# Attention keys kept per head with the other head's rows zero, and a 64-column operand for the meta values

## The reference, cut to what matters

```
z = einsum('bhtd,bhsd->bhts', q_blk, k_pre) * d ** -0.5
valid = (s_pos < t_pos) & (s_pos >= PAD)
log_not = where(valid, log_sigmoid(-z), 0)
after = cumsum(log_not, axis=3, reverse=True) - log_not
a = where(valid, exp(log_sigmoid(z) + after), 0)
out = einsum('bhts,bhse->bhte', a, v_pre)
```

## Time and profile before

| what | value |
|---|---|
| median of 3 runs | 2059.4 us (2056.85 to 2059.65) |
| the profiled execution | 2060.28 us, span 2058.5 us |
| TensorE matmuls | 1997.3 us busy, 97% of the span |
| VectorE | 1095.7 us, 53% |
| ScalarE | 710.2 us, 35% |
| GpSimd | 14.6 us, 1% |
| mean granted TensorE clock | 0.976 |
| chain that ended last | 85% on TensorE, 8% VectorE, 4% ScalarE |

### The profile page before, as it was taken

The page is one execution under the profiler, slowest core; times in us unless marked ns, Lnnn a source line. Parts: engine busy times, 40 slices in busy tenths (PEclk is TensorE's granted clock), DMA queues, the critical chain, the costliest instruction groups (busy, mean ns, idle before and its releaser), DMA issues.

```text
span 2058.5 us, 25213 instructions
## 1 busy us (share of the span) xinstructions
PE 1997.3 (97%) x10194; PEld 1671.5 (81%) x10194; DVE 1095.7 (53%) x1346; ACT 710.2 (35%) x845; POOL 14.6 (1%) x10
## 2 busy tenths in 40 slices
PE   7999999989999999999999999999999999999996
PEld 6878888878989888898768888887898768888885
DVE  3444646454364554636554454454699664545445
ACT  5554646533232232333332222223423442222222
POOL 0000000000000000000000000000000000000000
PEclk9888989989999999999999999999999999999998
DMA  4001101012212222212312232222122112232231
GB/s 166 23 23 39 62 20 61 21 55 99 87 68 82 71 82 92 81 63 80 124 64 82 102 102 82 102 102 82 61 83 82 42 61 94 90 102 102 82 103 41
DMA packets 23474, 157.53 MB, mean 77 GB/s; under 512 B 2672, under 2 KB 3056, under 8 KB 5360
## 3 DMA queue, kind: packets, MB, share of 16 engines
q1 hardware_dynamic: 23408, 156.59, 22.1%
HBM read 154.48 MB, written 2.10 MB: 76 GB/s over the span
## 4 chain that ended last, share of the span: by engine, by line
PE 85%; DVE 8%; ACT 4%; issue 2%; DMA 1%; DVEq 0%; SPq 0%; ACTq 0%
PE psum L464 27%; PE psum L465 26%; PE psum L466 26%; PE psum L596 2%; PE psum L518 2%; DVE z L1291 2%; DVE normed L1291 1%; DVE h L1320 1%; PE psum L584 1%; ACT w_hi L856 1%; DVE w_lo L1284 1%; ACT std L856 1%; DMA w_raw<-in_units 0%; PE psum L617 0%; ACT X_hi L856 0%
## 5 line engine op out<-in xcount | busy, mean ns | idle before, releaser
L464 PE MATMUL psum<-X_hi,w_hi 128*128 128x512 f32 (+1 forms) x1632 | 603.4, 370 | 5.9 <-DVE X_lo L1300 5.0
L465 PE MATMUL psum<-X_lo,w_hi 128*128 128x512 f32 (+1 forms) x1632 | 596.3, 365 | 0.0
L466 PE MATMUL psum<-X_hi,w_lo 128*128 128x512 f32 (+1 forms) x1632 | 595.5, 365 | 0.0
L856 ACT ACTIVATE w_hi<-w_raw 128x2048 fp32r<-128x2048 f32 x140 | 267.4, 1910 | 411.8 <-PE psum L466 395.3
L1284 DVE TENSOR_TENSOR w_lo<-w_raw,w_hi 128x2048 fp32r<-128x2048 f32 x138 | 315.9, 2290 | 144.4 <-ACT w_hi L856 144.4
L464 PEld LDWEIGHTS psum<-X_hi,w_hi 128*128 128x128 f32 x1632 | 307.7, 189 | 64.2 <-issue 6.7
L465 PEld LDWEIGHTS psum<-X_lo,w_hi 128*128 128x128 f32 x1632 | 307.6, 189 | 49.2 <-issue 2.2
L466 PEld LDWEIGHTS psum<-X_hi,w_lo 128*128 128x128 f32 x1632 | 307.2, 188 | 49.4
L1429 DVE TENSOR_TENSOR acc<-acc,psum 128x512 f32<-128x512 f32 x216 | 142.0, 684 | 86.7 <-PE psum L466 86.7
L464 PE MATMUL psum<-M_hi,w_hi 128*128 128x512 f32 x352 | 136.9, 389 | 0.0
L465 PE MATMUL psum<-M_lo,w_hi 128*128 128x512 f32 x352 | 136.9, 389 | 0.0
(11 more groups left out here) (237 smaller groups left out, 2658.4 us busy)
## 6 DMA issues: line engine op xcount, KB each, us to landing
w_raw<-in_units SPq DMA_DIRECT2D x140, 1024.0 KB, 4.8
h<-in_xfm SPq DMA_DIRECT2D x4, 528.0 KB, 5.4
h<-in_xfm SPq DMA_DIRECT2D x1, 2112.0 KB, 7.5
decay<-in_dec SPq DMA_DIRECT2D x4, 512.0 KB, 4.7
out<-h SPq DMA_DIRECT2D x4, 512.0 KB, 2.8
rot<-in_consts SPq DMA_DIRECT2D x1, 528.0 KB, 11.6
acc<-in_consts SPq DMA_DIRECT2D x1, 448.0 KB, 9.0
vec<-in_vecs SPq DMA_DIRECT2D x1, 108.0 KB, 3.7
```

What stands on the lines that cost most here:

```text
L464: nc.tensor.matmul(dst, w2[0], x2[0], start=first, stop=False, skip_group_check=True)
L465: nc.tensor.matmul(dst, w2[0], x2[1], start=False, stop=False, skip_group_check=True)
L466: m = nc.tensor.matmul(dst, w2[1], x2[0], start=False, stop=last, skip_group_check=True)
L856: return nc.scalar.activation(out_, in_, f, **kw)
```

## The change

`K_hi` and `K_lo` get a further dimension, the head r: in the part for head r only that head's 64 rows are written, and the other 64 rows are zero. They are cleared once, by four memsets on GpSimd at the start, and never written again. `scores` multiplies over all 128 rows of the keys of head r and of the queries (both heads' rows). `key_hi` and `key_lo` write each head's rows by an instruction of their own, on 64 partitions.

`XM_hi` and `XM_lo` have 64 columns (X's first 32, twice) in place of 128, so the meta part of the value strip writes 64 PSUM partitions. `VM`, `VM_hi` and `VM_lo` are worked on in 64 partitions, and GpSimd clears the upper 64 partitions of `VM_hi` and `VM_lo` at the start. TensorE waits for all six memsets (`keys_padded`) ahead of its first call of `scores`; the memset of `acc` is queued behind them. `KM`, `KM_hi`, `VM`, `VM_hi` and `VM_lo` move to a place in SBUF that is otherwise used later by `sig`.

```diff
--- before.py
+++ after.py
@@ -37,6 +37,7 @@
 FULL = META + SEQ
 HALF = FULL // 2
 X_PITCH = 576
+XM_COLS = 64
 UNIT = 2048
 RET_HEADS, RET_DK, RET_DV = 4, 256, 512
 QUADS = 4
@@ -177,25 +178,27 @@
 
     rot = sb("rot", [P, 2, FULL])
     mixer = ExitStack()
+    quad_small = ExitStack()
+    KM = sb("KM", [P, P], F32, quad_small)
+    KM_hi = sb("KM_hi", [P, P], F32R, quad_small)
+    VM = sb("VM", [P, 2, P], F32, quad_small)
+    VM_hi = sb("VM_hi", [P, 2, P], F32R, quad_small)
+    VM_lo = sb("VM_lo", [P, 2, P], F32R, quad_small)
+    quad_small.close()
     sig = sb("sig", [P, 2, FULL], where=mixer)
 
     quad = ExitStack()
     Q_hi = sb("Q_hi", [P, 2, SEQ], F32R, quad)
     Q_lo = sb("Q_lo", [P, 2, SEQ], F32R, quad)
-    K_hi = sb("K_hi", [P, 2, SEQ], F32R, quad)
-    K_lo = sb("K_lo", [P, 2, SEQ], F32R, quad)
+    K_hi = sb("K_hi", [P, 2, 2, SEQ], F32R, quad)
+    K_lo = sb("K_lo", [P, 2, 2, SEQ], F32R, quad)
     V_hi = sb("V_hi", [P, 2 * BLOCKS, 3, SB_DH], F32R, quad)
     V_lo = sb("V_lo", [P, 2 * BLOCKS, 3, SB_DH], F32R, quad)
-    XM_hi = sb("XM_hi", [P, DT, P], F32R, quad)
-    XM_lo = sb("XM_lo", [P, DT, P], F32R, quad)
+    XM_hi = sb("XM_hi", [P, DT, XM_COLS], F32R, quad)
+    XM_lo = sb("XM_lo", [P, DT, XM_COLS], F32R, quad)
     XM2 = sb("XM2", [P, DT, 2, META], F32R, quad)
-    KM = sb("KM", [P, P], F32, quad)
     KM_x = sb("KM_x", [P, 2, META], F32, quad)
-    KM_hi = sb("KM_hi", [P, P], F32R, quad)
     KM_lo = sb("KM_lo", [P, P], F32R, quad)
-    VM = sb("VM", [P, 2, P], F32, quad)
-    VM_hi = sb("VM_hi", [P, 2, P], F32R, quad)
-    VM_lo = sb("VM_lo", [P, 2, P], F32R, quad)
     sp = sb("sp", [P, PACKED], F32, quad)
     sp_hi = sb("sp_hi", [P, PACKED], F32R, quad)
     sp_lo = sb("sp_lo", [P, PACKED], F32R, quad)
@@ -282,6 +285,7 @@
     x_loaded = sem("x_loaded")
     decay_loaded = sem("decay_loaded")
     memset_done = sem("memset_done")
+    keys_padded = sem("keys_padded")
     stored = sem("stored")
 
 
@@ -294,8 +298,8 @@
     post_done = sem("post_done")
 
 
-    qk_act = Steps(sem("qk_act"), ["K_hi", "KM_hi", "Q_hi"])
-    qk_dve = Steps(sem("qk_dve"), ["K_lo", "KM_part", "KM", "KM_lo"])
+    qk_act = Steps(sem("qk_act"), ["K_hi0", "K_hi1", "KM_hi", "Q_hi"])
+    qk_dve = Steps(sem("qk_dve"), ["K_lo0", "K_lo1", "KM_part", "KM", "KM_lo"])
     mk_act = Steps(sem("mk_act"), ["m_abs", "m_exp", "m_ln", "m_hi", "am_exp", "am_hi"])
     mk_dve = Steps(sem("mk_dve"), ["m_sp", "m_lo", "am_lo"])
     mk_pe = Steps(sem("mk_pe"), ["m_scores", "m_rows", "y_meta"])
@@ -447,6 +451,17 @@
         nc.gpsimd.memset(ones[:, :], 1.0).then_inc(ones_ready, 1)
         pool.wait_ge(x_lo_ready, DT)
         nc.gpsimd.memset(KM[:, :], 0.0).then_inc(memset_done, 1)
+        pool.wait_ge(memset_done, 1)
+        for r in range(2):
+            other = slice(SB_DH * (1 - r), SB_DH * (2 - r))
+            for n, x in enumerate((K_hi, K_lo)):
+                if r or n:
+                    pool.wait_ge(keys_padded, 2 * r + n)
+                nc.gpsimd.memset(as_f32(x[other, :, r, :]), 0.0).then_inc(keys_padded, 1)
+        for n, x in enumerate((VM_hi, VM_lo)):
+            pool.wait_ge(keys_padded, 4 + n)
+            nc.gpsimd.memset(as_f32(x[XM_COLS:P, :, :]), 0.0).then_inc(keys_padded, 1)
+        pool.wait_ge(keys_padded, 6)
         pool.wait_ge(cmat_ready, 1)
         nc.gpsimd.memset(acc[:, :, :], 0.0).then_inc(memset_done, 1)
 
@@ -546,7 +561,7 @@
             for nb, col, x in parts:
                 for k in range(DT):
                     end = x is parts[-1][2] and k == DT - 1
-                    mm3(psum[:, at.bank(s) + nb, col:col + 256], (x[0][:, k], x[1][:, k]),
+                    mm3(psum[0:x[0].shape[2], at.bank(s) + nb, col:col + 256], (x[0][:, k], x[1][:, k]),
                         (w[0][:, k, :], w[1][:, k, :]), k == 0 and col == 0, k == DT - 1,
                         (strip_done, 1) if end else None)
 
@@ -575,12 +590,10 @@
             pe.wait_ge(strip_free, at.strip(s) + 1)
             if not (type(g) is int and g == 0):
                 pe.wait_ge(hd_act.sem, hd_act.at("a_part2", g - 1))
-            rows = slice(SB_DH * r, SB_DH * (r + 1))
-
             for b in range(BLOCKS):
                 dst = psum[:, 4 + KEY_BANK[b], KEY_COL[b]:KEY_COL[b] + KEY_LEN[b]]
-                mm3(dst, split(K_hi, K_lo, rows, t, slice(b * P, (b + 1) * P)),
-                    split(Q_hi, Q_lo, rows, t, slice(b * P, SEQ)), b < 3, False)
+                mm3(dst, split(K_hi, K_lo, ALL, t, r, slice(b * P, (b + 1) * P)),
+                    split(Q_hi, Q_lo, ALL, t, slice(b * P, SEQ)), b < 3, False)
                 m = nc.tensor.matmul(psum[:, 4 + KEY_BANK[b], KEY_COL[b]:KEY_COL[b] + P],
                                      cmat[:, C_IDENT, :], cmat[:, C_BLOCKED, :], start=False, stop=False,
                                      skip_group_check=True)
@@ -690,6 +703,7 @@
         unit(at, 0, 0, "P", SEQ, from_x, [1])
         pe.wait_ge(cmat_ready, 1)
         pe.wait_ge(quad_ready, 6)
+        pe.wait_ge(keys_padded, 6)
         scores(0, 0, at, 1, 0)
         meta_scores(0, 0)
         quad_body(Place("quad_first"), 0, False, True)
@@ -956,7 +970,9 @@
 
         def key_hi(t, at, s, p):
             strips(at, s)
-            a(K_hi[:, t, :], psum[:, at.bank(s), :], ACT.Copy).then_inc(*qk_act.step("K_hi"))
+            for r in range(2):
+                own = slice(SB_DH * r, SB_DH * (r + 1))
+                a(K_hi[own, t, r, :], psum[own, at.bank(s), :], ACT.Copy).then_inc(*qk_act.step(f"K_hi{r}"))
             act.wait_ge(qk_dve.sem, qk_dve.at("KM", p))
             a(KM_hi[:, :], KM[:, :], ACT.Copy).then_inc(*qk_act.step("KM_hi"))
 
@@ -972,7 +988,7 @@
                 .then_inc(*v_act.step(f"V_hi{half}"))
             if half == 0:
                 act.wait_ge(strip_free, at.strip(0) + 1)
-                a(VM_hi[:, :, :], VM[:, :, :], ACT.Copy).then_inc(*v_act.step("VM_hi"))
+                a(VM_hi[0:XM_COLS, :, :], VM[0:XM_COLS, :, :], ACT.Copy).then_inc(*v_act.step("VM_hi"))
 
         def y_hi(t, p):
             act.wait_ge(y_out, p + 1)
@@ -1021,8 +1037,8 @@
             a(x[:, :, 1, :], ones[:, 0:SB_DH].unsqueeze(1).broadcast_to([P, 2 * BLOCKS, SB_DH]), ACT.Copy,
               scale=0.0).then_inc(quad_ready, 1)
         for x, y in ((XM_hi, X_hi), (XM_lo, X_lo)):
-            a(x[:, :, :].rearrange("p k (j m) -> p k j m", j=4),
-              as_f32(y[:, :, 0:32]).unsqueeze(2).broadcast_to([P, DT, 4, 32]), ACT.Copy).then_inc(quad_ready, 1)
+            a(x[:, :, :].rearrange("p k (j m) -> p k j m", j=2),
+              as_f32(y[:, :, 0:32]).unsqueeze(2).broadcast_to([P, DT, 2, 32]), ACT.Copy).then_inc(quad_ready, 1)
         first_hi(1)
         key_hi(0, at, 0, 0)
         query_hi(0, at, 1)
@@ -1384,9 +1400,11 @@
             v.tensor_tensor(Y_lo[:, t, :], Y[:, :], as_f32(Y_hi[:, t, :]), ALU.subtract).then_inc(y_lo_ready, 1)
 
         def key_lo(t, at, s, p):
-            dve.wait_ge(qk_act.sem, qk_act.at("K_hi", p))
-            v.tensor_tensor(K_lo[:, t, :], psum[:, at.bank(s), :], as_f32(K_hi[:, t, :]), ALU.subtract)\
-                .then_inc(*qk_dve.step("K_lo"))
+            for r in range(2):
+                own = slice(SB_DH * r, SB_DH * (r + 1))
+                dve.wait_ge(qk_act.sem, qk_act.at(f"K_hi{r}", p))
+                v.tensor_tensor(K_lo[own, t, r, :], psum[own, at.bank(s), :], as_f32(K_hi[own, t, r, :]),
+                                ALU.subtract).then_inc(*qk_dve.step(f"K_lo{r}"))
 
 
             KM_rows = KM[:, 0:64].rearrange("p (r m) -> p r m", r=2)[:, :, 0:META]
@@ -1416,10 +1434,12 @@
                 ins.then_inc(strip_free, 1)
                 return
             ins.then_inc(*v_dve.step("V_lo0"))
-            v.tensor_tensor(VM[:, :, :], psum[:, at.bank(0) + 1, 0:2 * P].rearrange("p (t c) -> p t c", t=2),
-                            mask_v[:, :].unsqueeze(1).broadcast_to([P, 2, P]), ALU.mult).then_inc(strip_free, 1)
+            own = slice(0, XM_COLS)
+            v.tensor_tensor(VM[own, :, :], psum[own, at.bank(0) + 1, 0:2 * P].rearrange("p (t c) -> p t c", t=2),
+                            mask_v[own, :].unsqueeze(1).broadcast_to([XM_COLS, 2, P]), ALU.mult)\
+                .then_inc(strip_free, 1)
             dve.wait_ge(v_act.sem, v_act.at("VM_hi", i))
-            v.tensor_tensor(VM_lo[:, :, :], VM[:, :, :], as_f32(VM_hi[:, :, :]), ALU.subtract)\
+            v.tensor_tensor(VM_lo[own, :, :], VM[own, :, :], as_f32(VM_hi[own, :, :]), ALU.subtract)\
                 .then_inc(*v_dve.step("VM_lo"))
 
         def add_up(dst, at, s, ms):
```

## The result

The changed kernel takes 2012.7 us, the median of 4 runs (2012.39 to 2013.87), against 2059.5 before (2056.85 to 2060.54); the ratio is 0.9778, with a 95% interval of 0.9763 to 0.9793. It is 46.8 us faster. The forecast was 2015 us, 44.6 us faster than before.

The account below looks back on a forecast made before the run. TensorE's own stream was taken to bound the kernel, with its clock low in the quads. Savings of 44.3 us over the scores intervals plus 0.3 at the start gave 44.6, so 2015 us; eight-in-ten range 2009 to 2033.

Parts of the forecast that it names:

- The row changes: In each of 16 scores calls, eight changes between 64 and 128 rows go, saving 1.15 us per call.
- The clock: In the quads, eleven of fourteen half-clock stretches start at scores calls; mean clock there goes from 0.90 to about 0.98.
- Rival A: Clock falls aren't due to the half-filled array; only the row changes go, 18.4 us saved, 2041 us; chance 0.10.
- C: Rival: zero rows don't count as used, so scores falls stay and meta values add theirs; 2055 to 2068 us; chance 0.05.
- second head: Calls for a pair's second head: intervals fall to 11.55 us, saving 16.8 with a fall and 2.3 warm.
- first head: Calls for the first head, with meta products and value strip: to 12.41 us, saving 2.7 and 2.3.
- with a D unit, three: Calls inside a quad followed by output unit D: to 11.06 us by the VectorE chain, saving 11.0 us.
- fourth call: Call at 115.93, entered at low clock after a wait: second half of the stretch and row changes, 4.7 us saved.
- first call: Call at 44.09, behind an idle wait of 2.17 us that stays: 2.2 of 3.35 us saved.
- third and last: Calls with only warming products behind; the sp_lo wait takes back the clock's gain, 1.15 us each, 2.3 saved.
- The added work: Split key strips cost 0, a_lo keeping 0.9 us of room; six memsets hidden; at the start -0.3 us.
- The meta operand: 64-column operand in four value strips: taken as 0, between 1 us gained and 1.2 us for shape changes.

Follow-up runs that it names:

- E2: Kernel before, with the blocking product of a scores call over the same 64 rows as its score products, half the blocking left out: 2019.4 us.
- E3: Kernel after, with the blocking product over 64 rows and score products still over 128, so the row changes are back: 2038.2 us.
- E6: Kernel after, with every scores call's products issued twice, over 128 rows: 2053.3 us, one run.
- E5: Kernel before, with blocking product over 64 rows like the score products, and every scores call's products issued twice: 2066.6 us, one run.
- E10: Kernel after, with warming products in the idle waits and the second acc addition moved behind the first softplus steps in three D-unit quads: 2001.2 us.
- E8: Kernel after, with the value strip's meta part issued three times and 96 columns loaded in place of 64: 2076.5 us, one run.
- E7: Kernel after, with the value strip's meta part issued three times, 64 columns loaded: 2077.1 us, one run.

## Why the prediction was right

**The row changes.** 1.15 us were taken out of a call of 3.56. After, it is 2.35, so 1.21: the four blocking products cost 2.35 - 1.96 = 0.39 us and not the 0.45 that I gave them (0.06 us from start to start where I took 0.11, but for the last). About 0.1 more per call lies in the last product of outputs() ahead of it, which had one more change behind it. That makes some 0.16 us a change in the mean, an estimate from 1.3 us over eight. E2 and E3 take the gap away and bring it back with the score products' rows fixed: shown.

**The clock.** The forecast read off the fall's price and the place where it starts; the change takes away the half-filled array and the gaps at once, and the forecast didn't tell them apart. It was both together: each alone (E2, E3) leaves the clock at 1.00 in stretches where before it had 0.92. Why the two act together no run shows. Rival A fell with the result, C too. That no fall is left in after doesn't by itself show that zero rows count as filled, since E2 has none either without them; E3 shows it, with the zero rows and the gaps and no fall in fourteen calls where before has ten. E6 (zero rows) also had its clock back in 3.4 us at the first call where E5 (64 rows) took 13.7. The forecast counted eleven falls at calls, with the first call among them, whose fall stays in after; it is ten that the change removed. And rival A speaks of two stretches that begin in plain waits where the count above it has three.

The Trainium skill (TensorE: Matmul & The Clock Gate, What's actually happening) puts the clock down to how busy the array has been. The runs agree in that falls also come in waits (at the fourth call of after), but E3 shows that the small gaps alone aren't enough, and E5 against E6 that filled rows enter as well.

**The sum, by its terms.**

| intervals | forecast, saved | measured |
|---|---|---|
| second head: four with a fall, two warm | 16.8 + 2.3 | 16.9 + 2.5 |
| first head: one with a fall, two warm | 2.7 + 2.3 | 2.8 + 2.4 |
| with a D unit, three | 11.0 | 11.3 |
| fourth call | 4.7 | 5.1 |
| first call | 2.2 | 2.5 |
| third and last | 2.3 | 4.2 |

These are 44.3 and, before rounding, 47.8 us. All but the last line are right to 0.4 us. In the D quads the chain was the right one: forecast 11.06 with a wait of 1.7 us, measured 10.93 with 1.39, and E10 shows that the additions set it. But "a faster TensorE ends in a longer wait" did not come true: before it was 15.23 - 13.85 = 1.38 us, the same. The additions wait for TensorE's own D strips, so the chain got faster with it.

For the first and the fourth call the forecast gave the change part of a stretch, by judgement; that 2.2 and 4.7 came so near to 2.5 and 5.1 is partly luck. How long such a stretch lasts differs from run to run: E8, with like waits and 128 rows, has no fall at the first call (2.38 us) and one of 6.8 us at the fourth, where after has 3.4 at each.

The term that was mis-sized is the third and last call's, and its reason was half wrong. I said that a wait for sp_lo takes what the clock gives back. These are the two intervals, of the third and the last call, before and then after:

```profile
96.46:108.31 11.85, 11.85 (x71) 10.22 (x71) 5.15 (x10) 7.61 (x11) 0.00 (x0) 0.86 0.01 1
417.60:429.03 11.43, 11.43 (x70) 10.01 (x69) 8.34 (x11) 6.42 (x11) 0.00 (x0) 0.85 0.22 86
```

```profile
89.61:99.17 9.56, 9.31 (x72) 8.73 (x71) 4.24 (x8) 6.52 (x10) 0.00 (x0) 1.00 0.01 2
371.82:381.34 9.52, 8.90 (x70) 8.44 (x68) 7.97 (x11) 6.51 (x11) 0.00 (x0) 1.00 0.30 107
```

Before, there was no such wait at either: at the third call the 24 warming products filled the time at the low clock, then the full one, up to the first logs product at 108.31. After, the wait for sp_lo is there, but short: 9.56 - 9.31 = 0.25 us at the third call and 0.6 at the last, so the intervals save 2.3 and 1.9 us. At the third call the next wait, for m_lo, grew from 0.7 to 1.8 us, and from the third call to the fourth only 19.47 - 18.13 = 1.34 us are left, close to my 1.15. Most of the wait came one step later. At the last call nothing takes it back (16.77 instead of 18.68 us up to the outputs), and 0.8 more was saved than I said. So the two together brought 3.25 us and not 2.3, about 1 of the 3.1 us by which the span fell further than forecast; the rest is spread over the other terms.

**The added work.** The two K_lo halves take 1.41 us together where the whole took 0.69, so an instruction over half the partitions costs the same. In order of time on VectorE after, behind a key strip (TensorE's first product that uses a_hi and a_lo starts at 261.44):

```profile
253.48 1.41 DVE L1406 TENSOR_TENSOR K_lo<-psum,K_hi 64x512 fp32r<-64x512 f32 x2 [1.39 <-ACT K_hi L870]
...
259.15 1.50 DVE L1378 TENSOR_TENSOR a_lo<-a_f,a_hi 128x1280 fp32r<-128x1280 f32 x1 [2.00 <-ACT a_hi L870]
```

a_lo ends at 260.65, 0.79 us ahead; forecast 0.9. GpSimd ran the six memsets up to 38.5 us, as worked out:

```profile
33.81 0.95 POOL L460 MEMSET K_hi<- 64x1024 f32 x1
...
38.20 0.31 POOL L463 MEMSET VM_lo<- 64x256 f32 x1
38.56 3.54 POOL L466 MEMSET acc<- 128x4096 f32 x1
```

At the start I gave -0.3 us; the first call begins at 44.08 instead of 44.09. The XM copies gave 1.0, but the keys of both halves and then KM and the queries came one behind the other and used all of it. A single execution can't settle 0.3 us here: E3 and E7 have the same start and their first calls begin at 43.12 and 42.96.

**The meta operand** was given 0, between a gain of 1 and a cost of 1.2 for changes of shape. Here is the change of column count in after, on TensorE:

```profile
230.84 0.28 PE L481 MATMUL psum<-w_hi,XM_lo 128*64 128x256 f32 x1
230.96 0.40 PE L609 MATMUL psum<-sp_hi,cmat 128*128 128x512 f32 x1
231.19 0.39 PE L609 MATMUL psum<-sp_lo,cmat 128*128 128x512 f32 x1
```

0.12 us from the 64-column product to the next, as between its neighbours: no gap. The rule of the Trainium skill (TensorEngine Tiling (Array Packing), Key Properties) is that a change of tiling mode drains the array. The row changes agree with it (some 0.16 us each). The prediction took the 64 columns for such a change too, and there is nothing of it in the trace; whether a product with 64 columns loaded is in another mode at all no run shows.

## What to carry to other kernels

A product over 64 rows is here as long as one over 128 (0.23 and 0.24 us for 512 columns, E2 and after), but a change of row count between neighbours costs some 0.16 us; look at the distance between starts where the shape in the row changes, and make the shapes one, by zeros or by giving the odd product its neighbours' rows (E2 has most of the gain without zero rows, but leaves half of the blocking out). Where the granted clock falls, price the fall from two intervals of one shape, with and without it: here it was worth more than the gaps that helped to cause it. And once TensorE is faster, follow the chain that it then waits for: additions placed ahead of it were worth another 4 us, warming products in the waits 6 to 8.

## What the runs showed of the hardware

- Leaving out the first and the fourth call, with idle waits of 2 us ahead, the clock fell in calls mainly where half-filled rows and gaps came together. 64 rows with gaps: ten falls in fourteen calls, clock 0.92 over 234 us. 128 rows with the same gaps: none, 1.00 (E3). 64 rows without gaps: none in calls of 2.5 us, 1.00 (E2), two in calls of 4.8 us (E5).
- Half-filled rows, and gaps, hold a clock low that has already fallen: 10.2 us twice in E2, 10.2 and 13.7 in E3, against 3.4 and 3.4 in after; 13.7 and 17.1 in E5 against 3.4 and 6.8 in E6.
- A change between 64 and 128 rows costs some 0.16 us (3.56 us a call against 2.35). 64 of 128 columns loaded show neither: no gap at the change (0.12 us, after) and no fall in 8.4 us (E7).
